# The outset of a two-block transformer kernel in column halves, with slots of their own for the first seventeen weight loads

## The reference, cut to what matters

```python
cond = jax.nn.silu(c)
mod = cond @ w_ada[l] + b_ada[l]              # 1024 -> 9 * 1024
sh1, sc1, gt1, ... = split(mod, 9)            # first 1024: shift, next 1024: scale
u = rmsnorm(h, g_norm_ffn1) * (1 + sc1) + sh1
a, b = split(u @ w_ffn1_in, 2)                # 1024 -> 2 * 2816
h = h + 0.5 * gt1 * ((silu(a) * b) @ w_ffn1_out)
u = modulate(rmsnorm(h, g_norm_mix), sh2, sc2)
h = h + gt2 * token_mixing(u, ..., w_in, ...) # the stage called mix
```

## Time and profile before

| | |
|---|---|
| Median of three runs | 2670.45 us (2669.17 to 2670.98) |
| Profiled execution | 2668.95 us, span 2667.0 us |
| PE busy | 2425.0 us (91%), 14539 instructions |
| DVE, ACT, POOL busy | 51%, 32%, 8% |
| Chain that ended last | PE 66%, DMA 22%, DVE 4%, ACT 3%, issue 2% |
| Loads over the span | 591.62 MB, mean 222 GB/s |

### The profile page before, as it was taken

The page is one execution under the profiler, slowest core; times in us unless marked ns, Lnnn a source line. Parts: engine busy times, 40 slices in busy tenths (PEclk is TensorE's granted clock), DMA queues, the critical chain, the costliest instruction groups (busy, mean ns, idle before and its releaser), DMA issues.

```text
span 2667.0 us, 38184 instructions
## 1 busy us (share of the span) xinstructions
PE 2425.0 (91%) x14539; PEld 1778.1 (67%) x14540; DVE 1352.8 (51%) x2767; ACT 860.5 (32%) x1484; POOL 215.5 (8%) x168
## 2 busy tenths in 40 slices
PE   6999999999999999999987888889989988888787
PEld 4888888877678888787754444447755865544454
DVE  5766645442552244544653444336955574444445
ACT  4222335565332224322322111124367341211122
POOL 1000003000000000000011111110036001111110
PEclk9999999999999999999999898899999989989899
DMA  8666422112432232222489999995220349999987
GB/s 287 212 196 196 165 87 89 63 49 79 142 111 95 94 118 101 81 95 95 171 359 422 422 422 422 422 401 193 80 95 21 145 195 421 422 422 422 422 336 303
DMA packets 201771, 591.62 MB, mean 222 GB/s; under 512 B 10512, under 2 KB 126432, under 8 KB 152784
## 3 DMA queue, kind: packets, MB, share of 16 engines
q1 hardware_dynamic: 198496, 575.47, 56.1%
q0 software_dynamic: 2896, 14.47, 1.7%
q10 hardware_dynamic: 288, 0.43, 0.1%
HBM read 588.17 MB, written 7.41 MB: 223 GB/s over the span
## 4 chain that ended last, share of the span: by engine, by line
PE 66%; DMA 22%; DVE 4%; ACT 3%; issue 2%; SPq 1%; POOL 1%; DVEq 0%; ACTq 0%; POOLq 0%
PE bank L2181 40%; DMA arena<-in_exp_w 19%; PE bank L2550 7%; PE bank L2274 5%; DMA ring<-in_exp_w 2%; PE bank L2573 1%; SPq L609 1%; PE bank L2438 1%; DMA ring<-in_w_ffn_in 1%; DVE ring_low L1351 1%; PE bank L2785 1%; PE bank L2361 1%; PE bank L2591 1%; PE bank L2519 1%; PE bank L2754 1%
## 5 line engine op out<-in xcount | busy, mean ns | idle before, releaser
L2181 PE MATMUL bank<-parts 128*128 128x512 f32 x2560 | 795.9, 392 | 10.9 <-DVE parts L1628 4.8
L2181 PEld LDWEIGHTS bank<-parts 128*128 128x128 f32 x2560 | 482.2, 189 | 112.4 <-DVE ring_low L1351 6.5
L2181 PE MATMUL bank<-parts,ring_low 128*128 128x512 f32 x1280 | 500.5, 391 | 0.0
L2550 PE MATMUL bank<-ring,arena 128*32 128x256 f32 x2112 | 303.8, 447 | 83.6 <-DMA arena<-in_exp_w 83.6
L1351 DVE TENSOR_TENSOR ring_low<-ring,parts 128x2048 fp32r<-128x2048 f32 x109 | 245.1, 2251 | 179.2 <-ACT parts L838 170.2
L2550 PE MATMUL bank<-arena 128*32 128x256 f32 x2112 | 304.0, 447 | 32.2 <-issue 25.5
L838 ACT ACTIVATE parts<-ring 128x2048 fp32r<-128x2048 f32 x109 | 204.4, 1879 | 227.7 <-DMA ring<-in_w_ffn_in 115.4
L2181 PEld LDWEIGHTS bank<-parts,ring_low 128*128 128x128 f32 x1280 | 241.8, 189 | 51.0
L765 POOL COPY arena<-U 128x2048 f32<-128x2048 f32 x60 | 112.6, 1907 | 1762.5 <-PE bank L2550 1043.9
L2550 PEld LDWEIGHTS bank<-ring,arena 128*32 128x32 f32 x2112 | 141.0, 124 | 158.5 <-issue 135.0
L2550 PEld LDWEIGHTS bank<-arena 128*32 128x32 f32 x2112 | 142.1, 124 | 82.8 <-issue 49.1
(11 more groups left out here) (380 smaller groups left out, 3587.8 us busy)
## 6 DMA issues: line engine op xcount, KB each, us to landing
ring<-in_exp_w SPq DMA_DIRECT2D x188, 1024.0 KB, 18.9
arena<-in_exp_w SPq DMA_DIRECT2D x132, 1024.0 KB, 18.6
U<-in_exp_w SPq DMA_DIRECT2D x60, 1024.0 KB, 23.1
ring<-in_w_ffn_in SPq DMA_DIRECT2D x44, 1024.0 KB, 5.6
ring<-in_w_ada SPq DMA_DIRECT2D x36, 1024.0 KB, 5.5
ring<-in_w_ffn_out SPq DMA_DIRECT2D x20, 1024.0 KB, 5.1
ring<-in_w_in SPq DMA_DIRECT2D x18, 1024.0 KB, 5.0
ring<-in_conv_w_in SPq DMA_DIRECT2D x12, 1024.0 KB, 5.1
```

The lines of the kernel that those rows point to most:

```text
L2181: i = mm(o, a[:, cols[0], cols[1]], b, start=first_ and n == 0, stop=last_ and n == 2)
L2550: x = mm(bank[p][lanes_at:lanes_at + LANES, 0:2 * P].rearrange("p (w n) -> p w n", w=2), XW[:, k, LANES * (2 * p + e):LANES * (2 * p + e) ...
```

## The change

It does the following.

- Each of the first eight ada chunks holds four k of 512 columns instead of two k of 1024, in the order scale half 0, shift half 0, scale half 1, shift half 1. Four of them are loaded ahead of the first pair of feed-forward weights (now loads 4 and 5), four behind it (6 to 9).
- `slot_a` has a list of slots for loads 0 to 16; from 17 to 65 it is (n - 17) mod 6. The rule for `mix` is unchanged.
- DVE, not ACT, copies the turned x to `H`. `norm(0)` is replaced by written-out orders: DVE's `vector`, `first_low`, `normed`, `rest_of` and ACT's `first_norm`, with the weights of pair 0 rounded in halves (k 0 to 3, k 4 to 7).
- PE's `first_pair` multiplies k 0 to 3 of both column tiles of a, then two ada chunks, then k 0 to 3 of b with the sums of the third and fourth group in between, then k 4 to 7 of all four.
- The turning of `ln1_g` (L2171) and its evacuation move behind pair 0.

```diff
@@ ffn_at @@
-            return first["ffn0"] + (0 if c == 0 else 5 + 4 * (c - 1))
+            return first["ffn0"] + (0 if c == 0 else 8 if c == 1 else 5 + 4 * c)
@@ ada_chunks @@
-                    stream_a.append((flat(A["w_ada"], 2 * (a % 4), 2, D * (1 - a // 4), D), 2, D, "ada_mm", a + 1))
+                    stream_a.append((flat(A["w_ada"], 4 * (a % 2), 4, D * (1 - a // 2 % 2) + 512 * (a // 4), 512), 4, 512,
+                                     "ada_mm", a + 1))
-        ada_chunks(ADA_FIRST)
+        ada_chunks(4)
@@ ffn_stream @@
-                    ada_chunks(3 if c in (0, 10) else 2)
+                    ada_chunks({0: 6, 1: 3, 10: 3}.get(c, 2))
@@ slot_a @@
+            if n < ffn_at(0, 2):
+                return (0, 1, 2, 3, 4, 5, 0, 1, 2, 3, 0, 1, 2, 3, 0, 4, 5)[n]
             if n < first["mix"]:
-                return n % RING
+                return (n - ffn_at(0, 2)) % RING
@@ ACT @@
-            for k in range(KT):
-                act.wait_ge(sem("x_tp"), k + 1)
-                evac(H[:, k], bank[k % 4][:], "x_h")
+            def first_high(i, part):
...
+                C = slice(CHUNK // 2 * part, CHUNK // 2 * part + CHUNK // 2)
+                made = A_(high(i)[0][:, C], ring[:, slots[which][n], C], ACT.Copy)
...
+            def first_norm():
...
+                def row(g):
+                    act.wait_ge(sem("ada_mm"), 2 * g + 2)
...
+                    evac(AROW[:, g % 2], bank[4 + g % 2][:], "ada_row")
...
+                row(1)
+                first_high(0, 0)
+                act.wait_ge(sem("ada_mod"), 4)
+                tile(0)
+                tile(1)
+                first_high(1, 0)
+                tile(2)
+                tile(3)
+                first_high(0, 1)
+                first_high(1, 1)
+                row(2)
+                row(3)
+                act.wait_ge(sem("ada_mod"), ADA_FIRST)
+                for k in range(4, KT):
+                    tile(k)
@@ DVE @@
+            dve.wait_ge(sem("ada_mm"), 2)
+            nc.vector.tensor_copy(AROW[:, 0], bank[4][:]).then_inc(sem("ada_row"), 1)
+            vector(0)
+            for k in range(KT):
+                dve.wait_ge(sem("x_tp"), k + 1)
+                nc.vector.tensor_copy(H[:, k], bank[k % 4][:]).then_inc(sem("x_h"), 1)
+                if k == 6:
+                    dve.wait_ge(sem("keep"), 16)
+                    roots(0)
...
+            normed(0)
+            vector(1)
+            first_low(0, 0)
+            rest_of(0)
+            normed(1)
+            rest_of(1)
+            normed(2)
+            first_low(1, 0)
+            rest_of(2)
+            normed(3)
+            rest_of(3)
+            first_low(0, 1)
+            first_low(1, 1)
+            vector(2)
+            for k in range(4, KT):
+                normed(k)
+            vector(3)
+            for k in range(4, KT):
+                rest_of(k)
             ffn(0)
@@ PE @@
+            def first_pair():
...
+                pe.wait_ge(sem("opening"), 2)
+                for k in range(4):
+                    pe.wait_ge(sem("t_low"), tiles_at["ffn0"] + k + 1)
+                    for s in range(2):
+                        product(0, s, k)
+                ada_rows(4)
+                ada_rows(5)
+                pe.wait_ge(sem("opening"), 3)
+                for k in range(4):
+                    product(1, 0, k)
+                    if k == 1:
+                        ada_sums(2)
+                ada_rows(6)
+                ada_rows(7)
+                for k in range(4):
+                    product(1, 1, k)
+                    if k == 1:
+                        ada_sums(3)
+                pe.wait_ge(sem("w_low"), 2)
+                for s in range(2):
+                    for k in range(4, KT):
+                        pe.wait_ge(sem("t_low"), tiles_at["ffn0"] + k + 1)
+                        for which in range(2):
+                            x = product(which, s, k)
...
```

More of the change, by code:

```diff
@@ L400, in build @@
         first["ada"] = 0
-        ada_first = tuple(range(ADA_FIRST))
+        ada_first = tuple(a if a < 4 else a + 2 for a in range(ADA_FIRST))
         def ada_chunks(n):
@@ L903, in norm, with tile @@
                     tile_high(UM[0][:, KT - 1], U[:, KT - 1])
+            def first_high(i, part):
+                which, n = splits[i]
+                landed(act, which, n)
+                C = slice(CHUNK // 2 * part, CHUNK // 2 * part + CHUNK // 2)
+                made = A_(high(i)[0][:, C], ring[:, slots[which][n], C], ACT.Copy)
+                if part == 0:
+                    st.did(made)
+                else:
+                    made.then_inc(sem("w_high"), 1)
+            def first_norm():
+                act.wait_ge(sem("pool_step"), 4)
+                st.wait()
+                A_(small[:, 56:57], epsc[:, 0:1], ACT.Sqrt)
+                A_(small[:, 48:52], small[:, 60:64], ACT.Sqrt, scale=1.0 / D, bias=epsc[:, 0:1]).then_inc(sem("root"), 1)
+                def row(g):
+                    act.wait_ge(sem("ada_mm"), 2 * g + 2)
+                    if g >= 2:
+                        act.wait_ge(sem("ada_sum"), g - 1)
+                    evac(AROW[:, g % 2], bank[4 + g % 2][:], "ada_row")
+                def tile(k):
+                    act.wait_ge(sem("normed"), k + 1)
+                    A_(UP[0][:, k], U[:, k], ACT.Identity, bias=mod[:, k:k + 1]).then_inc(sem("t_high"), 1)
+                row(1)
[13 more added lines that the diff above has]
+                    tile(k)
             def ffn(i):
@@ L1103, in moe @@
                 return n
-            norm(0, lambda k: mod[:, k:k + 1], True)
-            act.wait_ge(sem("side_tp"), 1)
-            evac(LROW[0:64], bank[7][0:64, 64:64 + P], "side_out")
+            first_norm()
             ffn(0)
@@ L1424, in some_ada @@
                         now = a if it is None else it * 6 + a
-                        ada(ffn_at(0, c) + 2 + m, now, a, 0 if it is None else it * 32)
+                        ada(ada_at(c, m), now, a, 0 if it is None else it * 32)
                 def late_ada(c):
@@ L1600, in _ @@
             st.wait()
[L1601 to L1620, removed]
+            nc.vector.tensor_copy(CZ[:, :, 0:1], csil[:].unsqueeze(2)).then_inc(sem("opening"), 1)
+            def vector(g):
+                dve.wait_ge(sem("ada_sum"), g + 1)
+                c = KT * (1 - g % 2) + 4 * (g // 2)
+                TTn(mod[:, c:c + 4], bank[7][:, 4 * g:4 * g + 4], par[:, PC["b_ada"] + c:PC["b_ada"] + c + 4], ALU.add)\
+                    .then_inc(sem("ada_mod"), 2)
+                dve.wait_ge(sem("ada_mod"), 2 * g + 2)
+                if g % 2 == 0:
+                    C = slice(2 * g, 2 * g + 4)
+                    seq(STT(out=gains[:, C], in0=mod[:, c:c + 4], scalar=1.0, in1=par[:, PC["g_ffn1"] + 2 * g:PC["g_ffn1"] + 2 * g + 4],
+                            op0=ALU.add, op1=ALU.mult))
@@ L1621, in _, with first_low, normed @@
+            def first_low(i, part):
+                dve.wait_ge(*((sem("act_step"), TT + i + 1), (sem("w_high"), i + 1))[part])
+                n = slots["a"][splits[i][1]]
+                C = slice(CHUNK // 2 * part, CHUNK // 2 * part + CHUNK // 2)
+                TTn(ring_low[:, n, C], ring[:, n, C], high(i)[0][:, C].bitcast(F32), ALU.subtract)\
+                    .then_inc(sem(("opening", "w_low")[part]), 1)
+            def normed(k):
                 STT(out=U[:, k], in0=H[:, k], scalar=gains[:, k:k + 1], in1=bank[6][:],
@@ L1622, in _, with rest_of @@
                     op0=ALU.mult, op1=ALU.mult).then_inc(sem("normed"), 1)
[L1623 to L1626, removed]
+            def rest_of(k):
                 dve.wait_ge(sem("t_high"), tiles_at["ffn0"] + k + 1)
@@ L2116, in ada_rows, with ada_sums @@
                 landed(pe, "a", ada_first[a])
-                if a == 4:
-                    pe.wait_ge(sem("ada_row"), 2)
+                if a >= 4:
+                    pe.wait_ge(sem("ada_row"), a // 2 - 1)
                 w = chunk("a", ada_first[a])
[L2120 to L2124, removed]
-                x.then_inc(sem("ada_mm"), 1)
[L2127 to L2133, removed]
+                for k in range(4):
+                    x = mm(bank[4 + a // 2 % 2][32 * k:32 * k + 32, :], CZ[:, 4 * (a % 2) + k], w[:, k],
+                           start=(a % 2 == 0), stop=(a % 2 == 1))
+                x.then_inc(sem("ada_mm"), 1)
+            def ada_sums(g):
+                pe.wait_ge(sem("ada_row"), g + 1)
+                if g:
+                    pe.wait_ge(sem("ada_mod"), 2 * g)
+                for q in range(4):
+                    x = mm(bank[7][:, 4 * g + q:4 * g + q + 1], AROW[:, g % 2, P * q:P * q + P], ones[:, 0:1], start=True, stop=True)
                 x.then_inc(sem("ada_sum"), 1)
@@ L2183, in passes, with product @@
                 return i
+            def first_pair():
+                def product(which, s, k):
```

(18 more changed lines are left out.)

32 lines of the change are left out of this document (11 added, 21 removed).

## The result

The changed kernel takes 2676.48 us in the median of eight runs (2674.03 to 2678.06); the kernel before, on the same chip and in turns with it, 2668.37 us (2665.23 to 2670.98). The ratio is 1.0031, 95% interval 1.0023 to 1.0040: slower by 8.1 us, where 8.0 was forecast (as 2678 us, from the earlier median of 2670.45). The profiled execution took 2674.03 us with a span of 2672.2.

What follows compares the result with a forecast made beforehand. PE was taken as the bound, running alone for 206.92 us from 93.11 after an outset of loads, ACT and DVE. Terms 0.6 (outset to pair 1) + 7.4 (seam) = +8.0 on 2670.45 gave 2678 us, own range 2674 to 2682.

Steps and rivals of the forecast that it cites:

- The outset up to the last fold: Kernel start until PE last turns summed ada rows into columns: interleaved DVE and ACT steps, done at 46.5 us.
- rival C: Interleaved outset: PE's clock stays low all through it, last fold later by 2 to 3 us, total 2681 us; 15%.
- From the last fold to pair 1: PE and DVE after the last fold: pair 0 ends earlier but PE then stops; +0.6 us, ends -1.5 and +4.
- S: Time at which the last fold, PE's final turning of summed ada rows, is done: 46.5 us, not below 45.5.
- The DVE chain: DVE after the last fold: bias, tile, rests, ada 8 to 10, then the low part PE wants; ends at 70.3.
- the stop: PE in pair 1, waiting for DVE's low part from 65.0 to 70.3 us: 5.3 us idle, where it did not stop.
- The clock loss: PE's restart at 1.2 GHz after its new wait in pair 1: +1.5 us, at most 1.8.
- The 1.17 us stop: PE's old stall ahead of 93.11 us: goes, since DVE is ahead of PE in pair 2; -1.2 us.
- Rival A: Outset pays as it looks, -6.4 us, DVE not last at pair 1: 2668.0 us, or 2664 with free seam; 10%.
- The seam: First feed-forward's end to `mix`, near 406 us: load 66 waits for the last product, V +7.4 us, ends +3.9 and +8.4.
- Rival B: Seam hidden, `mix` loads landing before ACT asks: 2671 us, or 2675 with the seam at its lower end; 20%.
- nothing gives it back: Stages behind the seam: V, low parts and tiles keep their distances, so the +7.4 us stays to the end.

Runs made afterwards that it cites:

- e1: The changed kernel with ring slots renamed up to load 65, so the first mix load is freed as before the change: 2670.35 us, ratio 1.0011.
- e4: The changed kernel with POOL's constants (1.70 MB) sent only when V's first step is done: 2673.60 us, ratio 1.0023 to the kernel before.
- e3: The changed kernel with ACT's rounding of load 67 moved behind the eight tiles of norm(1): 2669.89 us, ratio 1.0010 to the kernel before.
- e5: e1 with DVE's ada chunk 10 moved behind the low part that PE waits for and tile 1: 2664.69 us, ratio 0.9986 to the kernel before.
- e7: e5 with the second low part and tile ahead of the last ada chunk in all pairs but the last: 2662.95 us, ratio 0.9981.
- e2: The kernel before with only the slots of loads 0 to 65 turned by one: 2676.14 us, ratio 1.0034.
- e9: The kernel before with e7's order of DVE alone, its outset, stream and slots the old ones: 2667.32 us, ratio 0.9999.
- e8: e7 with slots of loads 10, 11 and 14 changed so load 17 follows load 11: 2662.21 us, ratio 0.9975 to the kernel before.

## Why the prediction was right

**The outset up to the last fold** came to the forecast time, in part by luck. The steps were forecast for 28.6, 30.8, 33.2 and 35.4 and ended 0.6 earlier each; the last fold for 46.5 and ended at 46.51. In between, the 0.6 was lost: PE was through with the four steps at 36.5 instead of 36.8, since the first twelve or so of its matmuls ran at 1.2 GHz, and the fixed order behind them took 10.0 us instead of 9.7. The clock was low at the first products, as allowed for, and back from about 33 us on, before PE turned dense: rival C is out. Seven more executions with this outset had the last fold 0.0 to 1.2 us later (see the last section), so 46.51 is at the early end of what it does.

**From the last fold to pair 1.** The terms for the end of pair 0 (1.4, 0.5, 10.9, 0.3) add to S + 13.1, not to the 12.8 that I wrote; it ended 13.0 behind the fold, at 59.5, so pair 0 came 4.9 us earlier and not 5.2. The DVE chain was forecast to end at 70.3 and ended at 69.78; the stop for 5.3 us and was 4.60. PE's restart at 69.84 is then level with the same product of the kernel before (69.88 in its trace, where I had 70.0), not 0.3 behind. The clock loss is the term that I had too small: 1.5 (at most 1.8) against 2.1 here and 2.8 in e1. My price came from one stretch of 3.5 us at 0.50; the two restarts show 4.5 and 5.9. The 1.17 us stop went. Sum: 0.0 + 2.1 - 1.2 = +0.9, and the profile has +0.6 at the last product, the forecast's value: the restart was 0.3 earlier than forecast and the clock loss 0.6 larger, and the 0.3 that is left between this sum and the profile I can't place. That too is one execution. The last product of e4, e3 and e1, with the same outset, is 0.7, 1.8 and 2.1 late, and e1's time is 2.9 above the kernel before. So +0.6 is the low end of these four executions; the match of this term with one of them is partly luck. Rival A, the outset paying as it looks, is out in the changed kernel, where DVE's ada chunks end at S + 21.1 and PE asks at S + 18.7; e5 and e7 build its condition by moving one chunk behind the low part.

**The seam.** Load 66 waited for the last product, loads 67 to 69 stood behind it, ACT behind load 67. I had load 67 at 11.2 us after issue and it took 12.2, so V came at 422.14 instead of 420.8 (0.6 of that is the shift of the stage before); over the wait for V before, 8.2 instead of 7.4, just inside the upper end of 8.4. I had bounded POOL's traffic at 4.4 us and taken 3.5 of it; e4 shows 4.4. The Trainium skill's page "DMA: Bandwidth & Descriptors", section "Queues, rings and completion order", has the engines take turns between queues that have work; the trace agrees, since both sides are late, load 67 by 4.4 us and POOL's 1 MB by 3.6 (8.9 against 5.3). e2 shows that this one step is enough for a loss as large as the whole, and e3 that the path goes through ACT's order. Rival B is out by all three.

**What I had wrong without its hurting the sum** is that nothing gives it back. The shift of the changed kernel is 9.0 us at V's end, between 8.6 and 9.3 up to 1877 us, 7.0 at POOL's work at 2044.56 (2037.53 before) and 5.2 at the end, though in the medians it is 8.1. The changed kernel's profiled execution is the fastest of its eight. For 1.6 of what is lost the traces show the cause, and it is not the change. Near 2070 us PE resumes dense products after a stop, of 2.12 us in the kernel before and 2.50 in the changed one. Windows of 4 us from there, first of the kernel before, then of the changed kernel:

```profile
2065.24:2069.24 4.00, 4.00 (x11) 3.19 (x12) 4.00 (x5) 1.91 (x2) 0.00 (x0) 0.58 0.58 223
```

```profile
2072.64:2076.64 4.00, 4.00 (x18) 3.31 (x19) 4.00 (x5) 1.53 (x1) 0.00 (x0) 1.00 0.51 200
```

The mean of 0.58 is 3.4 us at 1.2 GHz, 1.7 us lost, and the shift goes from 7.4 to 5.8. In the ten other profiled executions the clock is 1.00 there, so the profile of the kernel before is the odd one. Where the rest goes is open; no run was made for it. So the agreement of 8.1 with 8.0 is partly luck: the seam was 0.8 above its term, the outset at or above its own, and a part of it was given back behind V.

## What to carry to other kernels

When a ring's slots are renumbered, look up the old holder of the first slot at every later stage, and when it comes free: a load that was 50 us ahead can end up behind the stage's last product, and here that alone cost as much as the whole change lost (e2). An engine's start moved forward pays only up to the next engine whose queue still holds the old order; count that queue from the same event before the gain is booked. Where one wait can't be avoided, see what stands behind it on its engine: moving one rounding of 1.9 us behind the tiles gave back 5.6 us of a stall of some 8 (e3).

## What the hardware showed that I had not expected

How long PE's clock stays at 1.2 GHz after a restart is no constant of this kernel. The stretches at 0.50 after PE resumed dense work lasted some 3.5 us at the first products of the kernel before, 4.5 after the changed kernel's stop and 5.9 after e1's, which was equally long (4.59 against 4.60). V, the same 64 products, took 15.61 us before and 16.93 in e1. It is not the new outset that makes it longer: e9, which has the old one, took 16.74. Windows of e1, then of the kernel before, in V:

```profile
419.50:421.50 2.00, 2.00 (x7) 1.61 (x6) 2.00 (x2) 2.00 (x4) 0.00 (x0) 0.54 0.00 0
```

```profile
415.40:417.40 2.00, 2.00 (x8) 1.63 (x7) 2.00 (x4) 2.00 (x5) 0.00 (x0) 0.71 0.04 8
417.40:419.40 2.00, 2.00 (x11) 1.76 (x10) 2.00 (x2) 2.00 (x4) 0.00 (x0) 1.00 0.00 0
```

e1 is at 1.2 GHz for 5.8 us of V (0.50 up to 419.50, and the window's mean of 0.54 leaves 0.2 us at full clock), the kernel before for 3.2 (by the mean of 0.71 the window from 415.40 has 1.2 us at half, behind 2.0 before it). Half of the difference is 1.3 us, all that V was longer. So a price taken from one restart carries about a microsecond of error either way.

The last fold also moved between executions by more than a microsecond, from 46.5 to 47.7 (e8). It is not the slots' names: e3 and e4 have the changed kernel's slots and outset, and DVE's first instruction behind the fold starts at 47.49 in e3 and at 46.55 in e4. The traces show the place. PE's 32 matmuls that turn x (L2232, in e8 L2236) start between 16.4 and 17.0 in the eight executions with this outset, and take between 5.24 and 6.45 us at a granted clock of 1.00 in all. The changed kernel, then e8:

```profile
16.51 5.24 PE L2232 MATMUL bank<-keep,arena 128*128 128x128 f32 x32 [0.52 <-DMA arena<-in_x]
```

```profile
16.84 6.45 PE L2236 MATMUL bank<-keep,arena 128*128 128x128 f32 x32 [0.53 <-DMA arena<-in_x]
```

The median of the 32 is 273 ns in the one and 417 ns in the other. From the end of this turning to DVE's first instruction behind the fold it is 24.6 to 24.9 us in all eight, so what moves the fold lies in the landing of x and in the turning. Why the same matmul takes longer in one execution no run tells.
